# A two-layer hybrid decoder trunk: filler matmuls, the merge summed on VectorE, reordered border operations, small matmuls padded to 128 rows

## What is computed

```python
for layer in range(DEPTH):
    u = rmsnorm(h, g_mix_pre) @ w_in                       # 1024 -> 7704
    y = stick_breaking(..), gla(..), mlstm(..), retention(..)   # four mixers, 256 wide each
    gates = sigmoid(merge_logits + b_merge)                # 4 x 1024 per token
    merged = sum(gates[n] * (y[n] @ w_branch[n]) for n in range(4))
    h = h + rmsnorm(merged @ w_out, g_mix_post)
    f = rmsnorm(h, g_ffn_pre)
    h = h + rmsnorm((silu(f @ w_gate) * (f @ w_up)) @ w_down, g_ffn_post)
```

## Time and profile before

| | |
|---|---|
| runs | 1014.41, 1015.05, 1016.66 us (median 1015.05) |
| the profiled execution | 1014.39 us, of which the span of instructions is 1012.6 |
| TensorE matmuls | 982.7 us busy (97%), 7664 instructions |
| weight loads | 931.5 us (92%) |
| VectorE | 592.2 us (58%) |
| ScalarE | 520.7 us (51%) |
| GpSimd | 128.1 us (13%) |
| DMA | 156.42 MB, mean 154 GB/s |
| mean granted TensorE clock | 0.991 |

### The profile page before, as it was taken

How to read it: one execution, slowest core, us unless ns; L and a number is a source line. 1 busy time by engine, 2 the same in 40 slices (tenths; PEclk the granted TensorE clock), 3 DMA queues, 4 the chain that set the end, 5 groups by cost and what they waited for, 6 DMA issues and landing times.

```text
span 1012.6 us, 19561 instructions
## 1 busy us (share of the span) xinstructions
PE 982.7 (97%) x7664; PEld 931.5 (92%) x7664; DVE 592.2 (58%) x870; ACT 520.7 (51%) x826; POOL 128.1 (13%) x106
## 2 busy tenths in 40 slices
PE   7999999999998999999989999999999899999997
PEld 5999888789997999999969998888999899999996
DVE  6556565346966655553465565744579656666443
ACT  4553754366466544454455437544754755454452
POOL 1000000002540222110000000000034212222010
PEclk9999999999999999999989999999999999999998
DMA  5874434246552655555545544344465536555551
GB/s 157 271 229 130 128 120 126 84 125 160 174 169 82 206 167 166 170 191 162 163 125 164 169 139 125 112 126 126 125 162 172 167 125 187 186 183 190 188 187 42
DMA packets 168523, 156.42 MB, mean 154 GB/s; under 512 B 9091, under 2 KB 167022, under 8 KB 168078
## 3 DMA queue, kind: packets, MB, share of 16 engines
q1 hardware_dynamic: 167598, 152.13, 48.7%
q10 hardware_dynamic: 672, 3.37, 1.0%
q0 software_dynamic: 192, 0.07, 0.0%
HBM read 154.50 MB, written 1.05 MB: 154 GB/s over the span
## 4 chain that ended last, share of the span: by engine, by line
PE 92%; DVE 4%; ACT 2%; issue 1%; DMA 1%; SPq 0%; DVEq 0%; ACTq 0%
PE banks L622 26%; PE banks L624 25%; PE banks L623 25%; PE banks L672 2%; PE banks L657 1%; PE banks L653 1%; PE banks L654 1%; PE banks L868 1%; DVE lo L1377 1%; PE banks L870 1%; ACT hi L1039 1%; PE banks L897 1%; PE banks L905 1%; DVE term L1648 1%; DMA xt<-in_x 1%
## 5 line engine op out<-in xcount | busy, mean ns | idle before, releaser
L622 PE MATMUL banks<-xh,hi 128*128 128x272 f32 (+1 forms) x1584 | 460.1, 290 | 2.4 <-DVE lo L1377 1.3
L1377 DVE TENSOR_TENSOR lo<-raw,hi 128x1024 fp32r<-128x1024 f32 (+1 forms) x290 | 356.4, 1232 | 174.8 <-ACT hi L1039 173.6
L624 PE MATMUL banks<-xh,lo 128*128 128x272 f32 (+1 forms) x1584 | 452.9, 286 | 0.0
L623 PE MATMUL banks<-xl,hi 128*128 128x272 f32 (+1 forms) x1584 | 452.8, 286 | 0.0
L1039 ACT ACTIVATE hi<-raw 128x1024 fp32r<-128x1024 f32 (+1 forms) x290 | 302.0, 1042 | 96.5 <-PE banks L624 58.0
L622 PEld LDWEIGHTS banks<-xh,hi 128*128 128x128 f32 x1584 | 298.5, 188 | 9.5 <-issue 6.6
L623 PEld LDWEIGHTS banks<-xl,hi 128*128 128x128 f32 x1584 | 298.0, 188 | 0.6
L624 PEld LDWEIGHTS banks<-xh,lo 128*128 128x128 f32 x1584 | 298.5, 188 | 0.0
L624 PE MATMUL banks<-ah,lo 128*128 128x272 f32 (+1 forms) x352 | 100.4, 285 | 0.0
L622 PE MATMUL banks<-ah,hi 128*128 128x272 f32 (+1 forms) x352 | 100.1, 284 | 0.0
L623 PE MATMUL banks<-al,hi 128*128 128x272 f32 (+1 forms) x352 | 99.9, 284 | 0.0
(11 more groups left out here) (252 smaller groups left out, 1176.4 us busy)
## 6 DMA issues: line engine op xcount, KB each, us to landing
raw<-in_w_in SPq DMA_DIRECT2D x54, 1024.0 KB, 5.2
raw<-in_ffn_w_gate SPq DMA_DIRECT2D x22, 1024.0 KB, 5.3
raw<-in_ffn_w_up SPq DMA_DIRECT2D x22, 1024.0 KB, 5.3
raw<-in_ffn_w_down SPq DMA_DIRECT2D x16, 1024.0 KB, 5.1
raw<-in_w_out SPq DMA_DIRECT2D x8, 1024.0 KB, 5.2
raw<-in_w_in SPq DMA_DIRECT2D x12, 512.0 KB, 4.4
raw<-in_w_branch SPq DMA_DIRECT2D x12, 512.0 KB, 5.6
raw<-in_ffn_w_down SPq DMA_DIRECT2D x8, 768.0 KB, 4.3
```

What stands on the lines that cost most here:

```text
L622: mm(dst, wh, mh, start=start, stop=False)
L623: mm(dst, wh, ml, start=False, stop=False)
L624: return mm(dst, wl, mh, start=False, stop=stop)
L1377: tt(lo[g % 2][:, 0:k, f], raw[g % 2][:, 0:k, f], hi[g % 2][:, 0:k, f].bitcast(F32), ALU.subtract).then_inc(lo_ready, 2 if g in G_MIX else 1)
```

## The change

Filler matmuls: 8 instead of 4 at the start, and new ones behind the sums of squares of the four kinds of norm (4 behind the first, 4 behind the norm of a sub-layer's output, 3 behind the second layer's first norm). They write a PSUM bank that is free then; behind the feed-forward TensorE waits for the reader of that bank first. GpSimd's `merge` is gone; VectorE makes both sums of every tile, in place, and the weight rest of a tile follows them; the rest of a merged tile is taken one tile behind. At the start ScalarE squares x in four pieces as they land, and the first half of weights is rounded and rested before the norm's root. In `add_sublayer` the first add goes ahead of the second scaling, and before the feed-forward each rest stands ahead of its tile's neighbour's add. ScalarE rounds the fifth feed-forward half ahead of the second root; VectorE takes its rest between the first two gate tiles. Matmuls of 16, 36 and 64 rows get 128 by padding with zeros: `wgate`, `gl` and `gr_rows` have 128 partitions, and the second pair's meta values get tiles of their own (`v0b`, `v0c`), set to zero by VectorE.

```diff
@@ -227,7 +227,7 @@
-WARM_START = 4
+WARM_START, WARM_FIRST, WARM_NORM, WARM_PRE = 8, 4, 4, 3
@@ -411,6 +410,12 @@
+        def meta_values(mix, pair):
+            if pair == 0:
+                return M["v0"][:, mix, :]
+            return M["v0b" if mix in (SB, RET) else "v0c"][:, mix // 3 if mix in (SB, RET) else mix - GLA, :]
@@ -689,9 +694,11 @@
-                pe.wait_ge(ss_ready, 6)
-                for b, (at, n) in enumerate(((0, META), (KB1, P), (KB2, P))):
-                    last = mm(ps[:, at:at + n], cut["mean"][0:n, :], sq[0:n, b, 0:n], start=True, stop=True)
+                pe.wait_ge(ss_ready, 10)
+                mm(ps[:, 0:META], cut["mean"][0:META, :], sq[0:META, 0, 0:META], start=True, stop=True)
+                for b, at in enumerate((KB1, KB2)):
+                    for n in range(2):
+                        last = mm(ps[:, at:at + P], cut["mean"], sq[:, 1 + 2 * b + n, 0:P], start=n == 0, stop=n == 1)
@@ -731,7 +738,7 @@
-                close_tile(mm(open_tile(t)[:, 0:T], wgate[:, l, :], M["small"][0:16, :], start=True, stop=True), t)
+                close_tile(mm(open_tile(t)[:, 0:T], wgate[:, l, :], M["small"][:], start=True, stop=True), t)
@@ -864,8 +871,7 @@
-                both = head_rows[pair % 2]
-                mm(ops[:, 0:T], M["v0"][both, mix, :], M["pt0"][both, :], start=True, stop=False)
+                mm(ops[:, 0:T], meta_values(mix, pair), M["pt0"][:], start=True, stop=False)
@@ -992,14 +998,19 @@
                     mean_square(l, 0, 0)
+                    keep_warm(WARM_PRE)
                 else:
                     mean_square_first()
+                    keep_warm(WARM_FIRST)
                 run_steps(l, parts)
...
                 mean_square(l, 1, q_start(l))
+                keep_warm(WARM_NORM)
                 gate_up(l)
...
                 mean_square(l, 3, q_start(l))
+                wait_taken(pe, TILE[l]["gu"] + 2)
+                keep_warm(WARM_NORM)
 
@@ -1050,17 +1061,18 @@
-                ss, spare = sq[:, KT - 1, 0:3], (sub[:, 0:4, 0:256], sub[:, 4:8, 0:256])
+                ss, spare = sq[:, KT - 1, 0:5], sub[:].rearrange("p k t -> p (k t)")
...
-                fn(spare[0][0:META], xt[0:META, 0, :].rearrange("p (a c) -> p a c", a=4), ACT.Square, accum_out=ss[0:META, 0:1]).then_inc(ss_ready, 1)
-                act.wait_ge(x_loaded[0], 16)
-                act.wait_ge(x_loaded[1], 16)
-                for b in range(1, 3):
-                    act.wait_ge(ss_ready, b)
-                    fn(spare[b % 2], xt[:, b, :].rearrange("p (a c) -> p a c", a=4), ACT.Square, accum_out=ss[:, b:b + 1]).then_inc(ss_ready, 1)
-                for b, n in enumerate((META, P, P)):
-                    act.wait_ge(ss_ready, 3)
-                    fn(sq[0:n, b, 0:n], cut["ident"][0:n, 0:n], ACT.Copy, scale=ss[0:n, b:b + 1]).then_inc(ss_ready, 1)
+                fn(spare[0:META, 0:D], xt[0:META, 0, :], ACT.Square, accum_out=ss[0:META, 0:1]).then_inc(ss_ready, 1)
+                for n in range(2):
+                    act.wait_ge(x_loaded[n], 16)
+                    for b in range(1, 3):
+                        at = 2 * b - 1 + n
+                        act.wait_ge(ss_ready, 1)
+                        fn(spare[:, 512 * (at - 1):512 * at], xt[:, b, 512 * n:512 * n + 512], ACT.Square, accum_out=ss[:, at:at + 1]).then_inc(ss_ready, 1)
+                for at, n in enumerate((META, P, P, P, P)):
+                    act.wait_ge(ss_ready, 5)
+                    fn(sq[0:n, at, 0:n], cut["ident"][0:n, 0:n], ACT.Copy, scale=ss[0:n, at:at + 1]).then_inc(ss_ready, 1)
@@ -1255,7 +1267,7 @@
-                act.wait_ge(*((merge_step[l], m + 1) if m < KT - 1 else (half_late[l], 2)))
+                act.wait_ge(merge_step[l], m + 1)
@@ -1301,7 +1313,8 @@
                 for c in range(2):
-                    round_half(n + c)
+                    if c:
+                        round_half(n + 1)
                     gate_tile(c, t + c)
@@ -1333,8 +1346,8 @@
                     square_first()
+                    round_half(0)
                     root(l, 0, 0)
-                    round_half(0)
                     act.wait_ge(bias_loaded, 48)
@@ -1348,6 +1361,7 @@
                 round_ffn_x(l, q0)
+                round_half(2 * G_GU[l] + ROUND_AHEAD)
                 root(l, 2, q0)
@@ -1381,12 +1395,12 @@
+                if l == 0:
+                    rest_of_half(0)
...
-                    if l == 0 and k == 1:
-                        rest_of_half(0)
@@ -1400,14 +1414,31 @@
-                for k in range(KT + 2):
-                    if k < KT:
-                        tt(sub[:, k, q0:], sub[:, k, q0:], rstd[:, q0:], ALU.mult).then_inc(post_scaled[l], 1)
-                    if 0 < k <= KT:
-                        dve.wait_ge(post_scaled[l], n // 2 * KT + k)
-                        tt(hT[:, k - 1, q0:], hT[:, k - 1, q0:], sub[:, k - 1, q0:], ALU.add).then_inc(h_ready[l], 1)
-                    if k > 1 and behind:
-                        behind(k - 2)
+                def scale(k):
+                    tt(sub[:, k, q0:], sub[:, k, q0:], rstd[:, q0:], ALU.mult).then_inc(post_scaled[l], 1)
+                def add(k):
+                    dve.wait_ge(post_scaled[l], n // 2 * KT + k + 1)
+                    tt(hT[:, k, q0:], hT[:, k, q0:], sub[:, k, q0:], ALU.add).then_inc(h_ready[l], 1)
+                scale(0)
+                add(0)
+                scale(1)
+                if behind:
+                    add(1)
+                    behind(0)
+                for k in range(2, KT):
+                    scale(k)
+                    if behind:
+                        behind(k - 1)
+                        add(k)
+                    else:
+                        add(k - 1)
+                if behind:
+                    behind(KT - 1)
+                else:
+                    add(KT - 1)
@@ -1423,6 +1454,7 @@
+                nc.vector.memset(M["v0b"][:], 0.0).then_inc(pad_set[l], 1)
@@ -1439,12 +1471,12 @@
-                dve.wait_ge(pad_set[l], 3)
+                dve.wait_ge(pad_set[l], 5)
...
-                    ins = nc.vector.tensor_copy(M["v0"][quad_real[h], mix, h % 2 * HD:h % 2 * HD + HD], ps0[0:META, h * HD:h * HD + HD])
+                    ins = nc.vector.tensor_copy(meta_values(mix, h // 2)[quad_real[h], h % 2 * HD:h % 2 * HD + HD], ps0[0:META, h * HD:h * HD + HD])
@@ -1477,6 +1509,9 @@
                         stt(M["mqk"][:, t, :], src, tap, M["mqk"][:, t, :], ALU.mult, ALU.add).then_inc(conv_step[l], 1)
+                if j == 3:
+                    dve.wait_ge(conv_step[l], 16)
+                    nc.vector.memset(M["v0c"][:], 0.0).then_inc(pad_set[l], 1)
 
@@ -1642,25 +1677,24 @@
                     dve.wait_ge(merge_step[l], m - 1)
+                t = term[:, m % 2, :, q0:]
                 for pair in range(2):
...
                     n = slice(2 * pair, 2 * pair + 2)
-                    tt(term[:, m % 2, n, q0:], branch_banks[(2 * m + pair) % 3][:, :, 0:T - q0], by_branch[:, n, m, q0:], ALU.mult).then_inc(branch_free[l], 1)
+                    tt(t[:, n, :], branch_banks[(2 * m + pair) % 3][:, :, 0:T - q0], by_branch[:, n, m, q0:], ALU.mult).then_inc(branch_free[l], 1)
                 if m == KT - 1:
-                    last = term[:, m % 2, :, q0:]
-                    dve.wait_ge(branch_free[l], 2 * KT)
-                    tt(last[:, 0:2, :], last[:, 0:2, :], last[:, 2:4, :], ALU.add).then_inc(half_late[l], 1)
-                    rest_of_merged(l, m - 2)
-                    dve.wait_ge(half_late[l], 1)
-                    dve.wait_ge(ml_ready[l], KT - 2)
-                    tt(acc[:, m % 2, q0:], last[:, 0, :], last[:, 1, :], ALU.add).then_inc(half_late[l], 1)
-                else:
-                    rest_of_half(at + REST_AHEAD)
-                if m and m != KT - 2:
                     rest_of_merged(l, m - 1)
+                dve.wait_ge(branch_free[l], 2 * m + 2)
+                tt(t[:, 0:2, :], t[:, 0:2, :], t[:, 2:4, :], ALU.add).then_inc(half_ready[l], 1)
+                dve.wait_ge(half_ready[l], m + 1)
+                if m >= 2:
+                    dve.wait_ge(ml_ready[l], m - 1)
+                tt(acc[:, m % 2, q0:], t[:, 0, :], t[:, 1, :], ALU.add).then_inc(merge_step[l], 1)
                 if m == KT - 1:
                     rest_of_merged(l, m)
-                    rest_of_half(at + REST_AHEAD)
+                rest_of_half(at + REST_AHEAD)
+                if 0 < m < KT - 1:
+                    rest_of_merged(l, m - 1)
 
@@ -1692,10 +1726,9 @@
-                for c in range(2):
-                    gate_tile(c, t + c)
-                    if c:
-                        rest_of_half(n + 1)
+                gate_tile(0, t)
+                rest_of_half(n + 1)
+                gate_tile(1, t + 1)
@@ -1716,10 +1749,11 @@
+            nc.vector.memset(wgate[:], 0.0).then_inc(misc_set, 1)
...
-            dve.wait_ge(misc_set, 5)
+            dve.wait_ge(misc_set, 6)
@@ -1770,27 +1804,13 @@
```

(17 more changed lines are left out.)

17 lines of the change are left out of this document (8 added, 9 removed).

## The result

The changed kernel takes 1002.55 us (median of 4 runs, 1001.41 to 1002.80) against 1015.86 (4 runs, 1014.41 to 1018.17) for the kernel before beside it. The ratio is 0.9865, with a 95% interval of 0.9843 to 0.9886: faster by 1.1 to 1.6%. 997.8 was forecast, so about a quarter of the expected gain is missing (nearly a third by the two profiled executions, 11.8 us of 17.2). The profiled execution took 1002.59 us with a span of 1000.8 (1012.6 before).

The account below looks back on a forecast made before the run. TensorE, busy 982.7 of 1012.6 us, was taken as the bound, so only what delays or slows it counts. Terms -5.6, -0.4, -0.5, -1.7, -2.7, -2.1, -4.0, -0.15 sum to -17.2 on 1014.39: 997.2, stated as 997.8; range 993 to 1005.5.

Parts of the forecast that it names:

- Small matmuls: Blocks of 16, 36 and 64 rows padded to 128 avoid changes of the array's shape: -5.6 us in all.
- Two gate blocks lose both: 0.8: With 128 rows the 16-row gate blocks lose both changes of shape, 0.40 us each: 0.8 us saved.
- 0.22 us in each of 16 values blocks, 3.5 us: With 128 rows each values block loses one of three changes of shape, saving 3.5 us in all.
- Head 0 gains one change: +0.3 in all: Head 0's exponents, among 64-row scores, get one more change of shape with 128 rows: 0.3 us lost.
- Rival C: Small blocks lose time to something else, such as half-wide matmuls; 128 rows give 1.9, not 5.6: 1001.5 us, chance 0.1.
- The start: Fillers lift the clock and early weights let TensorE begin sooner, so `first` ends at 27.3, not 31.7: -4.0 us taken.
- TensorE has 27 matmuls (3.4 us) behind the last: In `first`, TensorE's work left after VectorE's last tile, which sets the end at 27.3 us.
- Rival A: The start stays slow: fillers don't lift the clock or transposes lose it; 0 instead of -4: 1001.8 us, chance 0.2.
- Its rounded tile comes 0.24 earlier: -0.5: Norm before the feed-forward: adding tile 0 ahead of the second scaling starts TensorE earlier, -0.5 us over two layers.
- so all of it counts: -1.7: Layer 1's norm before the feed-forward: fillers hold the clock, and the whole loss of its fall is regained, -1.7 us.
- First weights, between the layers, merge: Earlier rounding of feed-forward weights -2.7; fillers and earlier sums between layers -2.1; merge on VectorE alone -0.4 us.
- Rival D: Slower than before: VectorE alone can't carry the merge, +30 us, ending at 1028; chance 0.04.

Follow-up runs that it names:

- gate_bank: Changed kernel with the two PSUM banks in front of the gate swapped and the second layer's gate reading 16 rows: 1000.93 us.
- fill_first: Changed kernel with six more fillers inside the first layer's `first` stage, where TensorE waits for VectorE: 1001.91 us.
- old_adds: Changed kernel with only VectorE's order in `add_sublayer` put back to that of the kernel before: 1001.8 us.
- no_fill: Changed kernel with the fillers of the kernel before, 4 at the start and none behind the norms: 1008.75 us.
- old_ffn: Changed kernel with only ScalarE's and VectorE's order at the fifth feed-forward half put back: 1004.19 us.
- old_start: Changed kernel with only the start's fillers undone, 4 ahead of the transposes and none behind the first sums: 1003.64 us.

## Why the prediction was right and where it was wrong

Right was what bounds the kernel and the sign of every term but the last; the new time lies in the range, 4.75 us above the forecast.

**Small matmuls, -5.6 against -3.25.** The step "Two gate blocks lose both: 0.8" failed. The loss by shape is real (0.39 by gate_bank), but a wait of nearly the same length stood behind it: 0.03 a layer came. The step "0.22 us in each of 16 values blocks, 3.5 us" was a little high in size (0.19) and wrong in assuming that each gain reaches the end: those of a layer's first two blocks were lost in the wait between them, so values gave 2.3. "Head 0 gains one change: +0.3 in all" was undersized: 0.33 a layer, 0.66, of which 0.15 a layer is lost overlap with the scores (at most 0.46 in the prediction). The lone exponents gave 0.39 each, 1.6 as said. Together -2.3 -0.06 -1.56 +0.66 = -3.3. Rival C (1.9 in all) named the wrong mechanism, and its size came nearer to the measured 3.25 than the forecast's 5.6; that is luck, since it blamed the half-wide matmuls and not the shape.

**The start, -4.0 against -2.2.** Up to the norm's root the steps hold: fillers end at 7.78 (8.0, though sixteen halves at 1.2 GHz would take 7.6 and not 7.3), sums at 13.59 (13.6), first product at 14.61 (14.8). What failed is "TensorE has 27 matmuls (3.4 us) behind the last": TensorE doesn't wait for the last tiles. VectorE's rest of weights delays tile 5, the last wait is for that tile (22.77), and behind it TensorE is the bound, with 49 matmuls, 6.1 us. That puts the end of `first` at 28.5 in fill_first, whose clock stayed up, not at 27.3, and the gain up to the gate at 3.0: about 1.0 of the missing 1.8 us is this step. The fall of the clock in the starved stretch adds 0.35. The remaining 0.5 is the execution itself, in which the first big matmul came at 15.78, against 15.30 in fill_first. Of the seven other runs with the same start, five reached the gate 0.9 to 1.5 us earlier than the profiled one and two 0.3 and 0.7 later. Over all ten profiles with eight fillers the gain up to the gate is 1.5 to 3.7 us, mean 2.9, so no execution came up to the forecast's 4.0. Rival A (the start stays slow) is out.

**The norm before the feed-forward.** "Its rounded tile comes 0.24 earlier: -0.5" gave about 0.1 a layer: the 0.24 is right for the first matmul, and the wait for VectorE's rest behind it takes half back (old_adds). In "so all of it counts: -1.7" the "all" failed: the held clock gave about 1.3. Of the fall's 3.4 us in the earlier trace rows, 0.8 lie before 807, where only the first three matmuls ran, the third of them waiting for VectorE at the full clock: at the first big matmul behind the norm the shift is -9.10, at the third -9.00, and -10.39 from the thirteenth on. The other 2.6 us at half rate are the 1.3. But the bound that I gave, that layer 0's clock may fall too, is what no_fill showed (2.48), so fillers are worth more than this pair of profiles shows: 6.2 us by the medians of no_fill and the changed kernel, nearly half of the whole gain.

**First weights, between the layers, merge.** 2.87, 1.94 and 0.23 against 2.7, 2.1 and 0.4; old_ffn confirms the first by itself with 2.90. The 2.1 between the layers was priced from two falls, which the profiled execution of the kernel before had; no_fill had one there and lost only 0.40, so how much of the 1.94 the fillers bring depends on the execution, and that the figure came so near is partly luck. In the merge the stall moved as said, from gathered_l to `lo`. Rival D (VectorE can't carry it) is out: its adds take 0.72 and 0.44 and TensorE waits nowhere before tile 6.

**The end of the kernel.** "Fast they save 0.4" did not come: the clock was down again from 996 on (0.60 over 2 us), and the last six transposes took 1.66 us as before. The line is +0.08 instead of -0.15.

**What would show it.** Clock 1.00, no wait at the third stage and 0.5 us for `lo` were seen. Values blocks of 1.72 for 1.68 and `first` ending at 29.4 for 27 were not quite.

## What to carry to other kernels

A loss that a timeline shows without a recorded wait can have a second, equally long one behind it: before it is priced, ask what the next instruction would wait for (here a bank that was still being emptied, marked only "issue"). A gain in one block counts only until the next wait on the same chain, and ScalarE's cheap reordering in front of that wait was worth half as much as all padding. Fillers paid here by holding the clock, and a fall cost only the part of it in which TensorE had work that was ready.

## What the runs showed of the hardware

- With the same filler matmuls from 1.25 us on, the clock rose at different times: 16 halves took 5.38 to 6.99 us in ten executions, which puts the rise between about 4.2 and 7.5, and the first big matmul moved with them, from 14.63 to 16.23. With eight halves, ending at 5.25, it never rose before the norm's sums (three executions: the kernel before, no_fill and old_start).
- Transposes neither lifted the clock (6.5 us of them in old_start, at 0.83 a tile) nor lost it: in all eleven executions that entered them at 2.4 GHz they ran over 4 us at 0.53 a tile and the sums behind them at full rate. At the end of the kernel, where waits stand between the transposes, it did fall among them (0.60 from 996 to 998).
The Trainium skill ("TensorE: Matmul & The Clock Gate", Part 4) says that transposes don't count as TensorE activity. That they did not lift it agrees; that the clock would be lost in them, which I had drawn from it, did not happen in these runs.
- Two changes of the array's shape around one fp32 matmul of 16 rows cost 0.39 us; fp32 matmuls of 36x32 and 64x32 ran in turns and saved 0.15 us against one after the other.
- Beside a GpSimd add VectorE's 128x272 subtraction takes 1.61 us instead of 0.43, and a rest of weights, which shares no tensor with the add, 1.79 instead of 1.22. The 1.61 is no fixed factor: that subtraction starts at 276.03 in the kernel before, inside this add of GpSimd, and ends 0.3 us behind the add's end. Taking the adds away changed the kernel's time by 0.3 us, since VectorE has slack.

```profile
275.06 2.28 POOL L1780 TENSOR_TENSOR half<-term 128x544 f32<-128x544 f32 x1 [2.83 <-DVE term L1648]
```
